# A new first stage and a second attention that stays in PSUM, in a fused two-layer decoder kernel

## The reference, cut to what matters

```
layer 0:  u = rms_norm(h);  q,k,v,qi,ki,wi = split(u @ w_in)        # 1024|256|256|512|64|8 columns
          q,k = rope(rms_norm per head);  qi,ki = rope
          score[t,s] = sum_h wi[t,h] * relu(qi[t,h].ki[s]);  keep the top 64 causal keys
          h += softmax(q.k / sqrt(128) over the kept keys) @ v @ w_out
          h += swiglu(rms_norm(h))                                  # 2816 hidden columns
shared:   k_sb, v_sb = split(rms_norm(h) @ kv_w)
layer 1:  z = (rms_norm(h) @ w_q) . k_sb / sqrt(128)                # strictly causal
          a = exp(log_sigmoid(z) + reverse exclusive cumsum over keys of log_sigmoid(-z))
          h += (a @ v_sb) @ w_out
          h += top-2-of-8 expert swiglu(rms_norm(h))
```

## Time and profile before

| | |
|---|---|
| median of three runs | 1248.77 us |
| the profiled execution | 1247.44 us, span 1245.4 us |
| TensorE busy | 1186.3 us (95%) |
| VectorE busy | 933.7 us (75%) |
| ScalarE busy | 791.2 us (64%) |
| GpSimd busy | 68.2 us (5%) |
| mean granted TensorE clock | 0.986 |
| chain that ended last | TensorE 88%, VectorE 6%, ScalarE 4% |
| HBM traffic | 288 GB/s over the span |

### The profile page before, as it was taken

How to read it: one execution, slowest core, us unless ns; L and a number is a source line. 1 busy time by engine, 2 the same in 40 slices (tenths; PEclk the granted TensorE clock), 3 DMA queues, 4 the chain that set the end, 5 groups by cost and what they waited for, 6 DMA issues and landing times.

```text
span 1245.4 us, 16878 instructions
## 1 busy us (share of the span) xinstructions
PE 1186.3 (95%) x6087; PEld 911.0 (73%) x6087; DVE 933.7 (75%) x869; ACT 791.2 (64%) x812; POOL 68.2 (5%) x83
## 2 busy tenths in 40 slices
PE   6967999999999898999999999999999999999897
PEld 6756999999897775767767776776776776776574
DVE  3684665455666458888888888889889888888796
ACT  5654553434447547677777777767767768677573
POOL 0000000000001204500000000000000000000110
PEclk9978999999999899999999999999999999999999
DMA  9528565643144139989999999999999999999980
GB/s 332 206 89 293 205 227 179 236 169 136 68 172 167 65 139 352 380 320 395 384 342 395 387 335 396 392 330 397 393 330 397 394 328 395 395 341 346 397 318 34
DMA packets 173085, 359.81 MB, mean 289 GB/s; under 512 B 6568, under 2 KB 47824, under 8 KB 173040
## 3 DMA queue, kind: packets, MB, share of 16 engines
q1 hardware_dynamic: 167568, 343.69, 75.5%
q0 software_dynamic: 4080, 15.34, 3.6%
q10 hardware_dynamic: 1392, 0.18, 0.1%
HBM read 347.65 MB, written 11.53 MB: 288 GB/s over the span
## 4 chain that ended last, share of the span: by engine, by line
PE 88%; DVE 6%; ACT 4%; issue 1%; DMA 1%; POOL 0%; ACTq 0%; SPq 0%; DVEq 0%
PE pair L461 28%; PE pair L463 27%; PE pair L462 27%; DVE up_lo L1399 1%; PE pair L822 1%; ACT up_hi L902 1%; DVE up_lo L1675 1%; ACT uT_hi L902 1%; DMA cst<-in_consts 1%; DVE dn_ring L1510 0%; DVE dn_ring L1521 0%; PE pair L575 0%; PE pair L584 0%; PE pair L784 0%; DVE top L1518 0%
## 5 line engine op out<-in xcount | busy, mean ns | idle before, releaser
L902 ACT ACTIVATE up_hi<-up_ring 128x2048 fp32r<-128x2048 f32 (+1 forms) x228 | 433.5, 1902 | 247.3 <-PE pair L463 247.2
L1675 DVE TENSOR_TENSOR up_lo<-up_ring,up_hi 128x2048 fp32r<-128x2048 f32 x176 | 402.4, 2289 | 92.6 <-ACT up_hi L902 90.0
L461 PE MATMUL pair<-up_hi,uT_hi 128*96 128x512 f32 (+2 forms) x880 | 351.0, 399 | 18.8 <-DVE up_lo L1399 5.0
L463 PE MATMUL pair<-up_hi,uT_lo 128*96 128x512 f32 (+2 forms) x880 | 346.3, 393 | 0.0
L462 PE MATMUL pair<-up_lo,uT_hi 128*96 128x512 f32 (+2 forms) x880 | 345.8, 393 | 0.0
L1780 DVE TENSOR_TENSOR dn_lo<-dn_ring,dn_hi 128x1024 fp32r<-128x1024 f32 x176 | 207.2, 1217 | 2.2 <-ACT dn_hi L902 2.1
L1399 DVE TENSOR_TENSOR up_lo<-up_ring,up_hi 128x2048 fp32r<-128x2048 f32 (+1 forms) x52 | 116.3, 2241 | 123.3 <-ACT up_hi L902 123.3
L902 ACT ACTIVATE dn_hi<-dn_ring 128x1024 fp32r<-128x1024 f32 x198 | 201.6, 1051 | 8.5 <-PE pair L463 7.8
L461 PEld LDWEIGHTS pair<-up_hi,uT_hi 128*96 128x96 f32 (+1 forms) x880 | 148.8, 169 | 77.3 <-issue 8.9
L463 PEld LDWEIGHTS pair<-up_hi,uT_lo 128*96 128x96 f32 (+1 forms) x880 | 148.5, 169 | 56.3
L462 PEld LDWEIGHTS pair<-up_lo,uT_hi 128*96 128x96 f32 (+1 forms) x880 | 149.0, 169 | 52.0
(11 more groups left out here) (263 smaller groups left out, 815.3 us busy)
## 6 DMA issues: line engine op xcount, KB each, us to landing
up_ring<-in_moe_w_gate_up SPq DMA_DIRECT2D x176, 1024.0 KB, 10.8
dn_ring<-in_moe_w_down SPq DMA_DIRECT2D x88, 1024.0 KB, 13.1
up_ring<-in_dense_w_gate_up SPq DMA_DIRECT2D x22, 1024.0 KB, 7.0
dn_ring<-in_dense_w_down SPq DMA_DIRECT2D x11, 1024.0 KB, 9.8
up_ring<-in_kv_w SPq DMA_DIRECT2D x4, 2048.0 KB, 8.1
y_rows<-q_T POOLq DMA_DIRECT2D x1, 6528.0 KB, 33.4
up_ring<-in_a_w_in SPq DMA_DIRECT2D x3, 2048.0 KB, 16.8
up_ring<-in_a_w_out SPq DMA_DIRECT2D x2, 2048.0 KB, 9.5
```

The costliest lines, as they stand in the source:

```text
L461: pe.matmul(ps, a_hi, b_hi, start=start, stop=False, skip_group_check=shared)
L463: return pe.matmul(ps, a_lo, b_hi, start=False, stop=stop, skip_group_check=shared)
L902: return act.activation(out_, in_, ACT.Copy, scale=scale)
L1675: dve.tensor_tensor(buffer(up_lo, p, 2048), raw_piece(2 * (T_MOE + i % STEPS) + p), buffer(up_hi, p, 2048).bitcast(f32), ALU.subtract).the ...
```

## The change

In the first stage:

- The five column tiles are cut anew (`IN_TILES`: 256, 328, 512, 512, 512 columns) and are multiplied as plain fp32, one matmul for each block, straight from the ring: the three fp32r matmuls go, and with them the ten splits on ScalarE and VectorE and the split of the activations.
- Only the identity is loaded ahead (on ScalarE's queue); x is loaded in column halves, the other constants after the first weight tile. Five matmuls on zeroed data run before any input is there.
- The heads' squares are taken from PSUM beside the copy. Query scaling goes into the exponent's scale, the query norm weight into the rotation tables and the key weight (GpSimd makes these).
- TensorE's order is finer: projections are cut in pieces, and transposes, index scores and logits put between them.
- The mask is added to the logits in PSUM by an fp32r matmul of the identity with the mask. VectorE takes row maxima and ScalarE exponentials straight from PSUM. The softmax goes in six groups of heads; heads 6 and 7 come last, inside the output product.
- Both output products take the first pieces of both column tiles first, then the second pieces.

In the second attention the mask is added by a matmul as well, the sum over keys accumulates onto the logits in the same PSUM pair (three pairs are in use), and GpSimd and the second pass of VectorE drop out. Abs and Exp of three head pairs run together, then their three Ln. The weighted sums of heads 0 to 3 come before the last value piece, those of heads 4 to 7 inside the output product.

```diff
+            pe.wait_ge(warm_set, 1)
+            for _ in range(5):
+                pe.matmul(bank[2][:, 0:256], work[:, 0:P], work[:, 0:256], start=True, stop=True)
+            pe.wait_ge(ident_in, 16)
+            uT_half(0, 0)
...
+            def project(j, t, ks=range(KD)):
...
+                    if t == 0:
+                        pe.wait_ge(up_in[j % RING], up_arrived(j))
...
+                    mm = pe.matmul(bank[(NT * j + t) % 4][:, 0:cols], uT_in[:, k, P * t:P * t + P], up_tile(j, cols)[:, k, :],
+                                   start=(k == 0), stop=(k == KD - 1))
...
+                    pe.matmul(ps[:, keys * m:keys * m + keys], q_T[:, i, P * t:P * t + P], kT_a[:, i // GROUP, 0:keys],
+                              start=(m % per_bank == 0), stop=False, skip_group_check=True)
...
+                    mm = pe.matmul(part, ident_r, bias[t].unsqueeze(1).to_broadcast([P, per_bank, keys]),
+                                   start=False, stop=True, skip_group_check=True)
...
+            for j in range(2):
+                for t in range(NT):
+                    project(j, t)
+            project(2, 0, range(0, 4))
+            index_T()
+            project(2, 0, range(4, 8))
             pe.wait_ge(idx_T_sb, 3)
             index_scores(0, range(8), 4)
             index_scores(1, range(4), 6)
...
+            project(2, 1)
+            pe.wait_ge(rel_done, 2)
+            index_scores(1, range(4, 8), 4)
+            project(3, 0)
             pe.wait_ge(rel_done, 6)
...
+            pe.wait_ge(qk_roped, 1)
+            heads_T(0, bank[4])
+            heads_T(1, bank[5])
+            project(3, 1)
+            project(4, 0, range(0, 6))
+            pe.wait_ge(qk_roped, 2)
+            heads_T(2, bank[6])
+            heads_T(3, bank[7])
+            project(4, 0, range(6, 8))
+            project(4, 1, range(0, 2))
+            pe.wait_ge(tables_set, 2)
+            pe.wait_ge(bias_done, 1)
...
+            for g in range(4):
+                logits(g)
+            project(4, 1, range(2, 8))
+            weights_T(0)
+            weights_T(1)
+            pe.wait_ge(qk_roped, 3)
+            heads_T(4, bank[0])
+            weights_T(2)
+            weights_T(3)
...
+            weighted_values(range(0, 4), 1)
...
+            logits(4)
+            logits(5)
...
-                pe.wait_ge(keep_done, j + 1)
-                if j >= 1:
-                    pe.wait_ge(expo_done, j)
+            def sticks_kept(j):
+
+                pe.wait_ge(sp_done, j + 1)
                 for i in range(2):
...
+                    ps, src = bank[2 * (j % 3) + i], sp[j][:, i, :]
+                    pe.matmul(ps[:, 0:TOK], upto, src[:, 0:TOK], start=False, stop=False, skip_group_check=True)
+                    pe.matmul(ps[:, P:TOK], minus_ones, src[:, TOK:TOK + P], start=False, stop=False, skip_group_check=True)
+                    mm = pe.matmul(ps[:, TOK:TOK + P], upto, src[:, TOK:TOK + P], start=False, stop=True, skip_group_check=True)
+                mm.then_inc(kept_ps, 1)
...
+            sticks_z(2)
             values(0)
             values(1)
...
+            sticks_kept(0)
+            sticks_kept(1)
+            sticks_kept(2)
+            sticks_z(3)
             values(2)
...
+            sticks_kept(3)
+            pe.wait_ge(v_sb, 2)
+            weighted_heads(0, 1)
             values(3)
...
+            query_roots(0, 6)
+            act.activation(one_out[:, :], ones[0:1, 0:1], ACT.Exp)
...
+            query_roots(6, 8)
+            act.activation(one_out[:, :], ones[0:1, 0:1], ACT.Exp)
+            output_part(0, 1)
...
-            log1p_exp(0)
-            log1p_exp(1)
+            act.activation(one_out[:, :], ones[0:1, 0:1], ACT.Exp)
+            for j in range(3):
+                abs_exp(j)
+            for j in range(3):
+                log1p(j)
```

More of the change, by code:

```diff
@@ L85, in program @@
         u = sb("u", [P, NT, DM])
+        with nc.sbuf_tensor("uT_in", [P, KD, TOK], f32) as uT_in:
+            pass
         uT_hi = sb("uT_hi", [P, KD, TOK], f32r)
@@ L160, in two_heads @@
             return v.rearrange("p (h c) -> p h c", h=2)
[L162 to L165, removed]
+        sp = [two_heads(v) for v in (work[:, 0:768], work[:, 768:1536], work[:, 1536:2304], take(768))]
+        minus_ones = take(P)
+        not_strict = hid_hi[:, 0:P]
+        ident_r = hid_hi[:, P:2 * P]
         d_silu = work[:, 0:1024].rearrange("p (b f c) -> p b f c", b=2, f=2)
@@ new lines, in weighted_heads @@
+            def weighted_heads(half, p):
+                for i in range(4 * half, 4 * half + 4):
+                    if i % 2 == 0:
+                        pe.wait_ge(stick_done, i // 2 + 1)
+                    ps = pair[p][:, TOK * (i % 4):TOK * (i % 4) + TOK]
+                    pe.matmul(ps, v_b[:, 0, HD * i:HD * i + HD], att[:, i, 0:TOK], start=True, stop=False)
+                    mm = pe.matmul(ps[:, P:TOK], v_b[:, 1, HD * i:HD * i + HD], att[:, i, TOK:TOK + P], start=False, stop=True)
+                mm.then_inc(o_ps, 1)
@@ L734, in first_half_T @@
                 stream_T(0, 1)
-            residual_product(T_BO, 0, first_half_T)
+            for n in range(2 * T_BO, 2 * T_BO + 4):
+                (_, part), half = tile_part(n), n % 2
+                pe.wait_ge(up_l, n + 1)
+                if half == 0:
+                    pe.wait_ge(o_l, 3 + part)
+                if n == 2 * T_BO:
+                    pe.wait_ge(stick_done, 4)
+                for t in range(NT):
+                    mm = token_columns(n, t, bank[2 * half + t])
+                    if t == 0 and part == 1:
+                        mm.then_inc(res_ps, 1)
+                        if half == 1:
+                            first_half_T()
+                    if t == 0 and n == 2 * T_BO:
+                        pe.wait_ge(v_sb, 4)
+                        weighted_heads(1, 2)
+                mm.then_inc(up_used, 1)
             pe.wait_ge(router_l, 1)
@@ L999, in relu_scores, with key_roots, query_roots @@
+            def key_roots():
+                act.wait_ge(consts_in, 16)
+                act.wait_ge(qk_ms, 2)
+                act.activation(qk_rs[:, :, NH:], qk_rs[:, :, NH:], ACT.Sqrt, scale=1.0 / HD, bias=eps).then_inc(qk_root, 1)
+            def query_roots(first, end):
+                act.wait_ge(qk_ms, 4 if first == 0 else 6)
+                act.activation(qk_rs[:, :, first:end], qk_rs[:, :, first:end], ACT.Sqrt, bias=hd_eps).then_inc(qk_root, 1)
             def relu_scores(n):
@@ new lines, in _ @@
+            for g in range(4):
+                exponentials(g)
+            proj_copy(4, 1)
+            head_squares(4, 1)
+            weights_T(1)
+            heads_T(4, bank[0])
+            query_roots(6, 8)
+            act.activation(one_out[:, :], ones[0:1, 0:1], ACT.Exp)
+            output_part(0, 1)
+            act.wait_ge(qk_rstd, 3)
+            exponentials(4)
+            exponentials(5)
+            up_piece(2 * T_OUT + 2)
+            weights_T(5)
+            output_part(1, 3)
```

775 lines of the change are left out of this document (382 added, 393 removed).

## The result

The changed kernel takes 1219.03 us (median of four runs, 1217.18 to 1219.37) beside 1249.58 us before (four runs on the same chip), a ratio of 0.9755 with a 95% interval of 0.9738 to 0.9773. The forecast was 1218.7. The profiled execution took 1219.33 us with a span of 1217.6.

The account below looks back on a forecast made before the run. TensorE's work plus its waits bound the two changed stages. Gains of 20.2 (first stage) and 9.9 us (second attention), 30.1 in all, took the profiled 1247.44 to 1217.3; 1.3 more for the median gave 1218.7, range 1211 to 1231.

Parts of the forecast that it names:

- Projection: First stage: input projection as plain fp32 takes 57.1 us of TensorE instead of 46.4, 10.7 us more.
- Start: First stage: first projection matmul at 10.8 us, between 10 and 12.5, with 1.5 us lost to a slow clock.
- Waits: First stage: 0.9 us for rotating heads 6 and 7, 0.9 for attention output, 0.7 for the last split; 1.9 margin.
- The close meeting: First stage: softmax of heads 0 to 5 beside the last six projection matmuls, normalised at 79.7 us, wanted at 80.2.
- Transfers at nothing: First stage: moved DMAs run ahead of TensorE throughout, a tile needing 5.9 us against 13.8 to be used; cost nothing.
- Second attention: Second attention: waits of 4.4 and 2.4 us and about 4 of lower clock go; 9.9 us gained, bounds 10.9 and 5.
- rival 2: First stage: softmax groups or fourth rotation miss their meeting with TensorE, costing 4 to 9 us; chance 0.19.
- the chain through ScalarE (3): Second attention stays a chain through ScalarE, with Exp and Ln tables changed five times, costing 5 us; chance 0.08.
- The table change at twice its load (4): Both attentions: each ScalarE table change costs twice its load, 2.6 us and about 6, giving 1227; chance 0.03.
- The early clock (5): First stage: clock is up before the first tile and all goes as planned, 1214 us or below; chance 0.10.
- fp32 at a lower clock (6): First stage: fp32 projection runs at the lower granted clock, 1276 us at 0.50 throughout, slower than before; chance 0.02.
- signs that I named for being wrong: TensorE waiting over 2 us in softmax groups, 512-column fp32 records over 0.45 us apart, or the experts' 770 us changing.

Follow-up runs that it names:

- the repetition: The changed kernel itself measured once more, with no edit, beside the kernel with the halved first tile on one chip: 1219.09 us.
- the run with all edits: Changed kernel with first tile halved, first attention-output half copied before the last square roots, two unused matmuls before the experts' third tile: 1216.85 us.

## Why the prediction came true, point by point

**Projection.** The first 72 records of the run with more matmuls on zeros go from 11.71 to the next instruction at 30.99: 19.3 us. My prices for them (32 records of 256 columns, 7.0; 32 of 328, 8.8; 8 of 512, 3.4) sum to 19.2. The guess of 0.55 for 328 columns was right, and fp32 at 0.86 per matmul of 512 columns is dearer than three fp32r at 0.70, as said. The Trainium skill ("FP8 and Floating Point Precision", TensorE Precision Notes) gives true FP32 four passes through the array. Four times the fp32r distance, my estimate from that, would be 0.93; the measured 0.86 decides. What a pass of it costs, no row here shows by itself.

**Start.** 11.17 us instead of 10.8, inside 10 to 12.5 (11.97 in the repetition). The slow start was 1.6 us where I took 1.5 without a row for it. That it came so near is in part luck: three of the six traces with this start show 2.9 to 3.0 us (22.28 to 22.43 against 19.4), more than the 2.7 that I had for all of it slow.

**Waits.** 0.8, 1.1 and 0.9 us where I had 0.9, 0.9 and 0.7, at the places named. What is left of the distance of 106.6, behind the work by my prices (57.1 and 43.8), the slow start and the waits, is 106.6 - 57.1 - 1.6 - 2.8 - 43.8 = 1.3 us for hand-overs; I had put 1.9 of margin. Dense stage at 117.80 against 117.6, 19.99 us gained against 20.2.

**The close meeting** (the softmax of heads 0 to 5) was looser than I wrote: VectorE normalised the last of the four groups by 81.17, not 79.7 (an exponential of 256 keys from PSUM starts every 0.54 us, not 0.49), but TensorE, which came at 81.13, first takes the two groups that were ready by 79.75, and the last one only behind the transposes of heads 6 and 7. I had set the end of the whole softmax against the first need. The two errors cancelled. That the cover is needed all the same, the run without it shows. The closest meeting was another one, that of the rotated keys and first queries, to which I had given 0.5 us (52.3 against 52.8). VectorE's last row of it, and TensorE's transposes:

```profile
53.43 0.22 DVE L1543 TENSOR_TENSOR u<-dn_ring 128x64 f32<-128x64 f32 x1
```

```profile
53.79 1.06 PE L553 MATMUL pair<-cst,u 128*128 128x128 f32 x8
```

It was ready 0.14 us before TensorE came.

**Transfers at nothing.** True in the result, but with less behind it than I thought: 1.8 us of slack at the output weights.

**Second attention.** 9.96 us gained, 9.9 forecast (the terms that I listed, 10.9 less 0.7, give 10.2; the last 0.3 had no source). The fourth pair, put at 0.5 us of slack, had 0.6. The split behind the last additions cost 0.88 us instead of 0.7.

**Rivals.** A close meeting missed (rival 2) and the chain through ScalarE (3) were made to happen by an edit each and cost 5.6 and 4.3 us, near the 4 to 9 and 5 that I had for them; in the changed kernel neither does. The table change at twice its load (4) is excluded. The early clock (5) needs matmuls until the tile lands and gives 1217.7 alone, 1216.5 with the tile halved, not quite the 1214 that I had for it. fp32 at a lower clock (6) doesn't occur: the windows read 1.00 from 15 us to the end of the stage.

**What I had not seen.** That the change doesn't touch the experts held for their work and not for their time. Of the signs that I named for being wrong this one came: their 770 us became 772. The sum of 30.1 us is met by the stages (29.85), but the profiled executions differ by 28.1 us only, so the one of the changed kernel took 1219.3 where I had 1217.3. I then added 1.3 us for the distance from the profiled execution to the median of before. In the changed kernel that distance is 0.3 us the other way, its profiled execution being the second slowest of the four. So 2.0 us too low and 1.6 too high nearly cancel in the median, 1219.03 against 1218.7. That part was luck.

## What to carry to other kernels

Lay the new order of the bounding engine out in time, with every meeting of it and another engine, before a change in order is costed: terms and waits were right to within a microsecond in the changed kernel's trace, though the change adds 12 us to that engine. Cost a wait of TensorE above 2 us at its length and a further 1.5 to 3 us of lower clock (waits of 2.3, 4.1 and 7.0 us brought 1.9, 1.5 and 3 here, the one at the start 1.6 or about 3.0), and fill an unavoidable wait with matmuls on zeros up to the instruction that ends it, not only ahead of it. When a stage is left with no waits, look for what is next before making its work cheaper: here it was a transfer with 1.8 us of slack that stood ahead of other work in ScalarE's order.

## What the runs showed of the hardware that I had not expected

The granted clock doesn't tell of every slow stretch: at the start without matmuls on zeros it reads 1.00 while records of 256 columns start as far apart as at the lower level (10 in 4 us; 20 in the run with all edits). The kernel before has the same: its column reads 1.00 from 16 to 21 us, where its fp32r matmuls start 0.244 us apart, and from 21 to 26 us, where they start 0.134 apart:

```profile
16.00:21.00 5.00, 5.00 (x21) 5.00 (x22) 1.58 (x5) 1.21 (x3) 0.00 (x0) 1.00 1.05 387
21.00:26.00 5.00, 5.00 (x38) 5.00 (x38) 1.38 (x1) 2.12 (x2) 0.00 (x0) 1.00 1.05 387
```

At a start, go by the distances.

A wait of one and the same length (1.96 to 2.0 us) at one and the same place was followed by the lower clock in five traces of twelve; in the changed kernel's two traces this cost 1.6 us. With the start, which takes 1.6 or about 3.0 us more than at full pace with nothing changed in its code, differences of 1.5 to 3 us between single executions of this kernel can be the clock alone.
